# A transformer-like stack on one core: the filler products of TensorE between the sublayers are left out

## What is computed

```python
# first block, layers 0 to 3 (mixers: hgrn2, differential attention, pooling, hgrn2)
h = h + 0.5 * rmsnorm(swiglu(rmsnorm(h, gn[0]), ffn1_w_in[i], ffn1_w_out[i]), gn[1])
hn = rmsnorm(h, gn[2])
m = mixer(hn)                       # by kind
h = h + rmsnorm(m, gn[3])
h = h + 0.5 * rmsnorm(swiglu(rmsnorm(h, gn[4]), ffn2_w_in[i], ffn2_w_out[i]), gn[5])
# second block, layers 0 and 1: the same frame, mixers: hybrid (SSD + attention), recurrent

def swiglu(x, w_in, w_out):         # 1024 -> 2 x 2816 -> 1024
    g, u = jnp.split(x @ w_in, 2, axis=-1)
    return (jax.nn.silu(g) * u) @ w_out
```

## Time and profile before

| | |
|---|---|
| timed runs | 3223.61, 3236.77 and 3239.11 us; median 3236.77 |
| profiled execution | 3224.06 us, span 3222.3 us |
| mean granted clock of TensorE | 0.987 |
| TensorE busy | 3133.9 us, 97% of the span |
| TensorE weight loads busy | 2728.6 us, 85% |
| VectorE busy | 2222.6 us, 69% |
| ScalarE busy | 1701.9 us, 53% |
| DMA | 534.79 MB, mean 166 GB/s |
| filler products, line 2115 | 216 records, 379 ns median |

### The profile page before, as it was taken

The page is one execution under the profiler, slowest core; times in us unless marked ns, Lnnn a source line. Parts: engine busy times, 40 slices in busy tenths (PEclk is TensorE's granted clock), DMA queues, the critical chain, the costliest instruction groups (busy, mean ns, idle before and its releaser), DMA issues.

```text
span 3222.3 us, 44753 instructions
## 1 busy us (share of the span) xinstructions
PE 3133.9 (97%) x18048; PEld 2728.6 (85%) x18048; DVE 2222.6 (69%) x2710; ACT 1701.9 (53%) x2098; POOL 4.5 (0%) x21
## 2 busy tenths in 40 slices
PE   9999999999999999999999999999787999999998
PEld 8888888888888888888888888888675888888887
DVE  7767675857585866776858586775855675866674
ACT  6565654545554653655547564654433554645553
POOL 0000000000000000000000000000000000000000
PEclk9999999999999999999999999999997999999999
DMA  6543454554355454454554355454330455554353
GB/s 228 194 168 124 155 185 172 192 188 152 123 191 184 181 185 144 177 189 171 195 183 144 131 183 184 177 188 172 136 124 1 163 190 183 183 184 156 144 194 120
DMA packets 75357, 534.79 MB, mean 166 GB/s; under 512 B 8480, under 2 KB 8608, under 8 KB 10784
## 3 DMA queue, kind: packets, MB, share of 16 engines
q1 hardware_dynamic: 75168, 532.07, 46.3%
HBM read 530.99 MB, written 1.05 MB: 165 GB/s over the span
## 4 chain that ended last, share of the span: by engine, by line
PE 92%; DVE 4%; DVEq 2%; ACT 1%; issue 1%; POOL 0%; POOLq 0%; ACTq 0%
PE pp L1985 36%; PE pp L1986 18%; PE pm L1985 8%; PE pp L2135 4%; PE pm L1986 4%; PE pp L2008 4%; PE pp L2038 2%; PE pp L1980 2%; PE pp L1979 2%; PE pp L1981 2%; PE pp L2010 2%; DVEq L405 0%; PE pm L1015 0%; PE pm L1028 0%; PE pp L372 0%
## 5 line engine op out<-in xcount | busy, mean ns | idle before, releaser
L1985 PE MATMUL pp<-xs,whi 128*128 128x512 f32 x4656 | 1633.7, 395 | 5.3 <-DVE tsum L1835 4.9
L1755 DVE TENSOR_TENSOR wlo<-raw,whi 128x2048 fp32r<-128x2048 f32 x465 | 1063.4, 2289 | 412.4 <-ACT whi L1563 411.8
L1986 PE MATMUL pp<-xs,wlo 128*128 128x256 f32 x4656 | 1304.0, 280 | 0.0
L1985 PEld LDWEIGHTS pp<-xs,whi 128*128 128x128 f32 x4656 | 872.8, 187 | 211.9 <-DVE tsum L1835 14.3
L1563 ACT ACTIVATE whi<-raw 128x2048 fp32r<-128x2048 f32 x465 | 887.3, 1911 | 292.4 <-DMA raw<-weights 291.7
L1986 PEld LDWEIGHTS pp<-xs,wlo 128*128 128x128 f32 x4656 | 880.3, 189 | 0.8 <-issue 0.2
L1653 ACT ACTIVATE corr<-pp 128x512 f32<-128x512 f32 x340 | 202.7, 596 | 620.8 <-PE pp L1986 594.6
L1985 PE MATMUL pm<-hs,whi 128*128 128x512 f32 x1120 | 400.3, 397 | 0.0
L1835 DVE TENSOR_TENSOR tsum<-pp,corr 128x512 f32<-128x512 f32 x327 | 225.5, 690 | 241.4 <-ACT corr L1653 241.0
L1986 PE MATMUL pm<-hs,wlo 128*128 128x256 f32 x1120 | 314.7, 281 | 0.0
L1985 PEld LDWEIGHTS pm<-hs,whi 128*128 128x128 f32 x1120 | 210.9, 188 | 47.8
(11 more groups left out here) (352 smaller groups left out, 3115.1 us busy)
## 6 DMA issues: line engine op xcount, KB each, us to landing
raw<-weights SPq DMA_DIRECT2D x503, 1024.0 KB, 4.8
raw<-weights SPq DMA_DIRECT2D x8, 256.0 KB, 7.2
h<-x_by_feature SPq DMA_DIRECT2D x4, 256.0 KB, 6.7
out<-h SPq DMA_DIRECT2D x4, 256.0 KB, 2.5
vec<-vectors SPq DMA_DIRECT2D x1, 264.0 KB, 2.8
lamrow<-diff_lambda SPq DMA_DIRECT2D x1, 128.0 KB, 11.4
skiprow<-ssm_d SPq DMA_DIRECT2D x1, 8.0 KB, 12.1
```

The source lines that it names most:

```text
L1755: v.tensor_tensor(wlo[:, slot, :], raw[:, slot, :], whi[:, slot, :].bitcast(F32), ALU.subtract).then_inc(sem("weights_lo"), 1)
L1985: mm(bank, whi[:, slot, c:c + P], x_k, start=start, stop=False)
L1986: return mm(bank[:, 0:T], wlo[:, slot, c:c + P], x_k[:, 0:T], start=False, stop=stop)
```

## The change

`first_of` calls `keep_clock` in the first sublayer alone. The 17 calls with 5 products each are gone. The call in the hybrid mixer stays. No wait, no semaphore, no DMA and no instruction of another engine is changed.

```diff
             def first_of(s):
 
-                keep_clock(5 if s["n"] else 7)
+                if s["n"] == 0:
+                    keep_clock(7)
                 first_pair(s["segs"][0], s["fill"])
```

## The result

| | before | after |
|---|---|---|
| timed runs, taken side by side | 3239.11 us median (3223.61 to 3241.66, 7 runs) | 3259.9 us median (3246.95 to 3275.25, 7 runs) |
| ratio | | 1.0076, 95% interval 1.0049 to 1.0103 |
| profiled execution | 3224.06 us, span 3222.3 us | 3270.2 us, span 3268.5 us |
| mean granted clock | 0.987 | 0.975 |

The change made the kernel slower, by 0.5% to 1.0%. The two profiled executions lie 46 us apart, more than the medians (20.8 us). So a part of these 46 us needs another explanation than the change, and the experiments come to it.

A forecast was written before the change was run, and what follows sets the result against it. TensorE was taken as the bound nearly everywhere, busy 97% of the span. Falls of 31.5 us less 2.5 us for mixers gave +29 us on 3230.9, so 3260 us; range on record 3234 to 3278.

The forecast's parts named there:

- The idle spell becomes 3.11 us in one piece: Between sublayers, ahead of line 2008: TensorE idles 3.11 us instead of 0.96; removing the fillers itself gains 0.
- 15 of 17 boundaries fall: At the gaps between sublayers the granted clock falls at 15 of 17, with 11 and 17 as ends.
- A short fall costs 1.7 us, a long one 2.9: Price of a clock fall at a boundary: 1.7 us for about 3.4 us, 2.9 us for about 7 us.
- Ten short and five long: Split of the 15 falls at boundaries: 10 x 1.7 + 5 x 2.9 = 31.5 us.
- 2.5 us off for the mixers: At the six boundaries that open a mixer, a later wait for VectorE may swallow some: 2.5 us off.
- Sum +29 us: Whole kernel: falls at the boundaries, less the part hidden in mixers, make it 29 us slower.
- The level of 3230.9 us: Mean of the profiled execution and three timed runs of before, taken as the level to which 29 us is added.
- The distance grows by nothing where the clock held: Sign: boundary-to-boundary distance grows by 1.7 to 2.9 us where the clock fell, by nothing where it held.
- The clock holds: Rival, chance 0.12: three or fewer falls at the boundaries, up to 5 us; time stays 3231 to 3237.
- Faster by the hybrid mixer's clock: Rival, chance 0.03: moving the hybrid mixer's half-clock stretches takes them away, 16 us, giving 3221.
- The change does less than it says: Rival, chance 0.02: boundary fillers are kept, line 2115 shows 216 records again, and the time of before.
- More than I priced: Rival, chance 0.06: all 17 boundaries fall, most of them long, 49 us, giving 3280.

The follow-up runs named there:

- the run with seven: Seven filler products instead of five at each boundary of the kernel before; ratio 1.0005 (0.9996 to 1.0014).
- The runs with one and three products: One or three filler products instead of five at each boundary of the kernel before; ratios 1.0046 and 1.0009.
- the third profile: The changed kernel, unchanged, profiled in a third execution and timed against the kernel before; ratio 1.0092 (1.0076 to 1.0109).
- the three later comparisons: Kernel before beside fillers at the first eight boundaries only (ratio 1.005), further fillers in the mixers (0.9938), and further fillers in the hybrid loop alone (0.9967).
- the five profiles with unfilled boundaries: Changed kernel three times (1.0076, 1.0065, 1.0092), fillers at the first eight boundaries only (1.005), the change on top of further mixer fillers (1.006).

## Why the prediction was right

The forecast was 3260 us, within 3234 to 3278, slower; measured 3259.9. That the number agrees so closely is luck in its sum, and it has to be taken apart.

- *The idle spell becomes 3.11 us in one piece, and its length doesn't change.* Right: 3.12 ahead of line 2008, 3.11 between the ends. The fillers themselves cost nothing, as the run with seven confirms.
- *15 of 17 boundaries fall.* Right, in three profiles of three. Sorting the idle spells of the trace of before by length carried this: 2.78 and 2.50 us fell, 1.78 fell and held. The runs with one and three products give the same order at the boundaries themselves, 14 and 2 of 17. There was luck in it: those two single spells fell in only 6 and 8 of eleven profiles, and in the first profile of the changed kernel neither did. Had they held in the one that I read, the case for a fall would have rested on the spells of the hybrid mixer alone.
- *A short fall costs 1.7 us, a long one 2.9.* Each too dear: 1.4 and 2.4. A short fall takes 8 records from a window that held 46 in 8 us, 8 x 8.0 / 46 = 1.4. I had priced it in the pooling and recurrent mixers. There a record's step goes from 216 to 427 ns at the lower level, so nearly half of a fall is lost. Behind a boundary the steps at full clock are about 233 and 118 ns and at the lower level 427 and 213, so that at most 45% is lost, 1.5 us of 3.4. And the long price took 1.1 us for idle, where one of its two rows, 2398 to 2405, has 1.87 us; by the same sum that is 2.6.
- *Ten short and five long.* 7 and 8, 14 and 1, 7 and 8 in three profiles. The share is the execution's own, so the term has a spread (219.2 to 226.3 us of openings, with 15 falls each) that I had not given it.
- *2.5 us off for the mixers, as a wait for VectorE that swallows some.* No such wait shows: the openings of mixers grow like the others, and the stretches of three of the six behind them keep their length to 0.2 us. What moves is falls inside a mixer. In the first profile of after, the pooling and the recurrent mixer each had one fall less than in before (1.6 and 1.7 us), and the hybrid mixer's stretch was 3.1 us longer; in the third profile the first two had all theirs. So the term had no ground, and made up for part of the dear prices.
- *Sum +29 us.* The openings measured +28.3, +21.2 and +28.0 in the three profiles. By timing, the ratio of 1.0076 is 25 us, and the medians differ by 20.8 us. So the effect was forecast 4 to 8 us too large.
- *The level of 3230.9 us.* Too low by as much: the seven runs of before taken beside the changed kernel have a median of 3239.11, 8.2 us higher. The two errors cancel. In the three later comparisons before stood at 3232.07, 3242.9 and 3223.67.
- *The distance grows by nothing where the clock held.* This sign was not met: from the ninth to the tenth boundary it is 192.2 us in the first profile of after, without a fall, and 190.1 in before. The 2.1 us are the pace of the products, which I had not reckoned with. The other signs came as named: 46 records on line 2115, 53.2 us of waits, a mean clock of 0.975.
- *Why runs of before lie 15 us apart.* I gave it to the hybrid mixer's stretch, redrawn in every execution. That sublayer does vary (312.4 to 319.0 us in five profiles with its fillers untouched and no fall at its opening), but the larger part can be what I had not seen at all: feed-forward sublayers of 190.1 or 192.2 us, twelve of them. The trace of before held it, since openings at 355.95 and 548.17 lie 192.2 us apart and those at 548.17 and 738.28 only 190.1; I had not compared them.
- *The rivals.* The clock holds: refuted at 15 of 17. Faster by the hybrid mixer's clock: not found; the sublayer takes 320.2 us, 1.4 of them the fall at its opening, against 315.7. The change does less than it says: line 2115 has 46 records, as named. More than I priced: not in a profile, but the slowest timed run of after, 3275.25 with the lowest granted clock of the seven, 0.972, may be near it.

## What to carry to other kernels

Products that compute nothing can pay for themselves on an engine that has to wait anyway: five of them in a gap of 3.1 us kept the next 11.6 us of real products from taking 13.0 to 14.2. To judge such a filler, sort the engine's idle spells by length and look at the granted clock behind each, in more than one profile, since one and the same spell falls in one execution and holds in the next; then count records in equal windows with and without a fall for the price; and look for the open waits of the same length elsewhere, which here were worth 0.6% more. When an effect of some 20 us is to be read from one profile of each kernel, compare stage by stage first: here the two profiles differed by 46 us, of which 19 came from the pace of products that the change leaves alone.

## What the runs showed of the hardware that was not expected

- The same products, at a granted clock of 1.00 and with no idle time, run at one of two paces: 463 or 455 records in 80 us, 190.1 or 192.2 us for a whole feed-forward sublayer. It changes from one feed-forward sublayer to the next, holds for the whole of a sublayer's first part, and never shows in the second; kernels with and without fillers have it. Its cause is open.
- At the boundaries the number of falls rises steeply with the idle spell: 0, 2, 14 and 15 of 17 at 0.96, 1.81, 2.69 and 3.12 us. A spell of 3.12 us can still pass without one, and a single spell of 2.6 to 2.8 us in the pooling mixer did so in 5 of eleven profiles.
- A fall at a boundary lasts 3.4 or 6.8 us. Long ones came with spells of 3.12 us (3.46 at the sixteenth boundary) and were absent from the 14 falls with 2.69 us. In the five profiles with unfilled boundaries, 68 falls, all 25 long ones began 0.67 to 1.75 us before the first product, and all short ones later.
